# Hybrid attention and short-convolution layer: turned value groups at other steps, another order of the attention step on three engines, and several waits and transfers moved

## The chip, the cores and the metric

The kernel runs on one core of one Trainium2 chip. The metric is device time in microseconds (us): before the change the median of three runs is 2747.36 us (2747.1 to 2748.34). A core has five engines with a queue each, which meet only at semaphores: TensorE (PE) multiplies matrices and turns tiles, VectorE (DVE), ScalarE (ACT) and GpSimd (POOL) work on rows, SyncE (SP) issues most transfers. Each engine takes its instructions in the order of its own program; what is late at the head of a queue holds back all behind it.

## The reference

```python
u = rms_norm(x, norm_mix_g)                       # x: (1, 2048, 1024) float32
q, k, v, bg, cg, hv = split(u @ w_in)             # each 512 wide
s = q_c @ k_c.T + bias[bucket(k_pos - q_pos)]     # 4 heads, 2 halves c of 64 columns each
a = softmax(s_0) - lam * softmax(s_1)
att = rms_norm(a @ v, subln_g) * (1 - 0.2)
conv = bg * short_conv(cg * hv, conv_w)           # width 3 over positions
x = x + concat(att, conv) @ w_out
z = rms_norm(x, norm_ffn_g)
x = x + (silu(z @ w_gate) * (z @ w_up)) @ w_down  # 2816 wide
out = rms_norm(x, final_g)
```

All is float32 within a tight bound. The kernel gets it from products of a rounded type: each operand is split into a high part (a copy that rounds, on ACT) and a low part (operand minus high part, on DVE), and a product is three matmuls: high by high, high by low, low by high.

## The kernel before

It has five stages, one after another on PE.

- **Input projection.** x is normalized in four blocks of 512 rows; each block has four tiles of 128 rows, which `scale_x` scales on DVE, `turn_u` turns on PE, and `split_u` splits on ACT and DVE. Between them stand the first three pieces of the product (`first_product`); `norm_block` is DVE's order within a block. Three further triples of 128 columns follow in a loop (q, k and v), then 4 loops for the convolution. `piece_staged` counts the pieces that DVE has taken out of a bank of PSUM (the memory PE writes to). Near the start the vector of relative bias is spread over the partitions, one matmul for each head (`spread_bias`), and kept by ACT (`keep_bias`).
- **Attention.** 64 steps, 16 for each of 4 heads, counted from 0; step t brings a tile of 128 queries to 2048 keys. In the tables that set the order within a step (one line for steps t % 4 = 0, 1, 2, 3; one table each for PE, ACT and DVE), `s0` to `s3` are the four score units of tile t on PE (4 matmuls of 512 columns each; the two halves of the keys for each of the two halves of a head), `S0` is the first unit of the next tile, `b0` to `b3` add the bias and keep the running minimum on DVE, `x0` and `x1` take the exponential of a 2048 wide row on ACT (`x1` of the tile before), `r` is a reciprocal on DVE. Then POOL scales and adds the two halves (`mixed_ready`). Two steps later the mixed tile is turned in four groups of 128x512 (`g0` to `g3`): 4 transposes on PE, the high part on ACT, the low part on DVE, in two banks of PSUM in turn, so that a group must be finished on DVE before the next but one can start on PE (`group_lo`). The values of a block of four tiles are multiplied in eight parts, `e0` to `e7`, of 6 matmuls each, in steps 1, 2 and 3 after that block; step 0 has none. `o`, `M`, `h`, `R` and `a` normalize a block. `step_groups` says which groups are turned in a step. Four of the groups of a head are its values v instead (tile `None`): quarter 0 in step 2, 1 in step 3, 2 in step 4, 3 in step 5, each behind the step's other groups.
- **Output projection.** 16 tiles of 128 rows (n = 0 to 15). SP loads the mixed tile n (`load_m`, two slots), ACT and DVE split it, PE multiplies, DVE adds x (`add_rows`), ACT squares, POOL takes the root, DVE scales (`norm_rows`), PE turns the result (`turn_z`) one tile later. `norm_rows(n)` stands behind `split_m(n + 2)` on DVE, and so does the square on ACT.
- **Gate and up**, 44 steps of 7 products with sums of blocks.
- **Down and final norm.** Four groups of 512 rows; each sums 22 chunks. `split_down` splits a chunk, `add_y`, `mean_y` and `norm_y` finish the rows, POOL stores them.

The steps around the change in code: `pe.wait_ge(piece_staged, ...)` ahead of the loops over triples and over the convolution; `dve.wait_ge(out_gain_loaded, 16)` ahead of the last product; `load_m` in SP's loop over n.

## Time and profile before

| | |
|---|---|
| median of three runs | 2747.36 us |
| the profiled execution, its own time | 2750.09 us |
| its span (first to last instruction) | 2748.1 us |
| TensorE's mean granted clock | 0.989 |
| input projection | 0 to about 568 us |
| attention | about 568 to 1205 us |
| output projection | about 1200 to 1405 us |
| gate and up | about 1405 to 2243 us |
| down and final norm | about 2243 to 2748 us |
| matmuls | 12280 |

All times below are of the one profiled execution, counted from the start of its span; its own time is 2.7 us over the median. A duration of PE is modelled and includes what overlaps with the next matmul, so what PE costs is read from the distance between starts. "[3.2 <-DVE x]" at the end of a line is how long the engine stood idle before it and what released it. PEclk is the share of full speed that TensorE's clock was granted.

### The profile page before, as it was taken

What the parts mean: (1) busy time and instruction counts of PE and PEld (TensorE: products, weight loads), DVE (VectorE), ACT (ScalarE), POOL (GpSimd) and SP (SyncE); (2) the same over time, 40 slices, a digit from 0 to 9 for tenths busy, and PEclk for the clock granted to TensorE, in tenths of its full rate; (3) what the DMA queues carried; (4) which work ended last, traced back from release to release, by engine and by line L of the source; (5) the groups of instructions that cost most, each with busy time, mean ns of one, the idle gap of its engine ahead of it and who ended that gap; (6) DMA issues with size and microseconds to landing.
All of it is one profiled execution on the core that took longest, in us unless ns stands there. A gap on an engine that the chain in (4) does not pass through costs nothing. (4 is left out here: it accounts for less than half of the span.)

```text
span 2748.1 us, 34348 instructions
## 1 busy us (share of the span) xinstructions
PE 2656.5 (97%) x12280; PEld 2177.7 (79%) x12280; DVE 1505.5 (55%) x2203; ACT 1020.8 (37%) x1429; POOL 501.1 (18%) x343
## 2 busy tenths in 40 slices
PE   7999999989999999999999999999999989999997
PEld 6788888867777777778888888878888878888886
DVE  5311122268878877854476656686666643534343
ACT  5210000047667766742243333343333322323232
POOL 1000000047777777720000000000000000000000
PEclk9999999999999999999999999999999999999999
DMA  6542111223031221047673222352222234556563
GB/s 183 147 126 82 58 38 38 61 62 75 25 76 47 62 61 31 24 146 222 216 232 115 76 84 91 103 165 73 88 85 79 88 123 137 183 172 201 155 200 113
DMA packets 260688, 298.30 MB, mean 109 GB/s; under 512 B 15200, under 2 KB 179552, under 8 KB 260608
## 3 DMA queue, kind: packets, MB, share of 16 engines
q1 hardware_dynamic: 255952, 287.24, 35.2%
q0 software_dynamic: 2304, 8.39, 0.7%
q10 hardware_dynamic: 2352, 1.64, 0.2%
q8 instruction: 46, 0.75, 0.1%
q14 instruction: 34, 0.28, 0.0%
HBM read 212.28 MB, written 84.93 MB: 108 GB/s over the span
## 5 line engine op out<-in xcount | busy, mean ns | idle before, releaser
L1826 PE MATMUL banks<-z_hi,w_hi 128*128 128x512 f32 x1116 | 434.5, 389 | 1.8 <-DVE u L1417 1.1
L1826 PE MATMUL banks<-z_hi,w_lo 128*128 128x512 f32 x1116 | 434.2, 389 | 0.0
L1826 PE MATMUL banks<-z_lo,w_hi 128*128 128x512 f32 x1116 | 434.2, 389 | 0.0
L1621 PE MATMUL projected<-u_t_hi,w_part_hi 128*128 128x512 f32 (+1 forms) x768 | 300.6, 391 | 3.2 <-DVE conv_y L1146 1.7
L1621 PE MATMUL projected<-u_t_lo,w_part_hi 128*128 128x512 f32 (+1 forms) x768 | 299.7, 390 | 0.0
L1621 PE MATMUL projected<-u_t_hi,w_part_lo 128*128 128x512 f32 (+1 forms) x768 | 299.6, 390 | 0.0
L719 POOL TENSOR_TENSOR exp<-exp,exp 128x2048 f32<-128x2048 f32 x64 | 295.5, 4617 | 5.3
L878 ACT ACTIVATE exp<-exp,neg_max 128x2048 f32<-128x2048 f32 x128 | 257.2, 2009 | 36.4 <-DVE neg_max L1288 35.3
L748 POOL TENSOR_TENSOR y_rstd<-y_mean,neg_half 128x1 f32<-128x1 f32 x16 | 8.7, 546 | 1319.5 <-DVE y_mean L1572 1319.5
L1826 PEld LDWEIGHTS banks<-z_hi,w_hi 128*128 128x128 f32 x1116 | 209.5, 188 | 46.9 <-issue 2.8
L1826 PEld LDWEIGHTS banks<-z_lo,w_hi 128*128 128x128 f32 x1116 | 209.5, 188 | 43.3
L1826 PEld LDWEIGHTS banks<-z_hi,w_lo 128*128 128x128 f32 x1116 | 209.5, 188 | 43.3
L980 ACT ACTIVATE w_hi<-w_sum 128x512 fp32r<-128x512 f32 x176 | 110.8, 632 | 328.1 <-PE banks L1826 321.1
L1883 PE MATMUL banks<-down_hi,hid_hi 128*128 128x512 f32 x704 | 217.9, 391 | 7.5 <-DVE down_lo L1560 7.5
L1883 PE MATMUL banks<-down_lo,hid_hi 128*128 128x512 f32 x704 | 217.7, 390 | 0.0
L1883 PE MATMUL banks<-down_hi,hid_lo 128*128 128x512 f32 x704 | 217.5, 390 | 0.0
L888 ACT ACTIVATE a_t_hi<-tile_turned 128x512 fp32r<-128x512 f32 x256 | 148.5, 601 | 157.9 <-PE tile_turned L1713 157.4
L1300 DVE TENSOR_TENSOR a_t_lo<-tile_turned,a_t_hi 128x512 fp32r<-128x512 f32 x256 | 172.1, 687 | 54.0 <-ACT a_t_hi L888 53.9
L1557 DVE TENSOR_TENSOR hid_lo<-hid_raw,hid_hi 128x512 fp32r<-128x512 f32 x88 | 60.9, 693 | 254.3 <-ACT hid_hi L1078 241.8
L1695 PE MATMUL scores<-k_sum,q_part_hi 128*128 128x512 f32 x512 | 178.8, 431 | 15.1 <-DVE neg_max L1288 8.5
L1288 DVE CUSTOM_DVE_ANT_0 exp<-scores,window,half_min 128x1024 f32<-128x1024 f32 x128 | 163.8, 1280 | 31.5 <-PE scores L1695 25.7
L1078 ACT ACTIVATE hid_hi<-hid_raw 128x512 fp32r<-128x512 f32 x88 | 55.5, 631 | 329.9 <-PE banks L1883 329.9
(154 smaller groups left out, 4557.1 us busy)
## 6 DMA issues: line engine op xcount, KB each, us to landing
down_raw<-in_w_down SPq DMA_DIRECT2D x88, 512.0 KB, 4.4
gate_raw<-in_w_gate SPq DMA_DIRECT2D x44, 512.0 KB, 4.8
up_raw<-in_w_up SPq DMA_DIRECT2D x44, 512.0 KB, 5.8
hidden_t<-hid_stage SPq DMA_DIRECT2D x88, 256.0 KB, 2.6
hid_raw<-hidden_t SPq DMA_DIRECT2D x88, 256.0 KB, 3.6
w_raw<-in_w_in SPq DMA_DIRECT2D x24, 512.0 KB, 5.1
projected_t<-stage SPq DMA_DIRECT2D x48, 256.0 KB, 2.5
q_part_hi<-projected_t SPq DMA_DIRECT2D x32, 256.0 KB, 4.5
```

The source lines that it names most:

```text
L719: nc.gpsimd.tensor_tensor(exp_0[:, slot_0], exp_0[:, slot_0], exp_1[:, slot_1], ALU.add).then_inc(mixed_ready, 1)
L878: nc.scalar.activation(rows, rows, ACT.Exp, scale=-1.0, bias=neg_max[:, t % 2, part:part + 1], accum_out=exp_sum[:, part, t % 16:t % 16 + ...
L888: nc.scalar.activation(dst, turned_bank(h, t, index), ACT.Copy).then_inc(group_hi, 1)
L980: nc.scalar.activation(w_slot[k][0][:, :, :], src, ACT.Copy).then_inc(w_hi_ready_2, 1)
L1078: nc.scalar.activation(hid_part[slot][0][:, :], hid_raw[:, slot], ACT.Copy).then_inc(f_hi_ready, 1)
L1288: nc.vector.tensor_tensor_reduce(out=rows[:, half * HALF:(half + 1) * HALF], in0=scores[:, unit % 2], in1=window[:, window_slice(t, half)] ...
L1300: nc.vector.tensor_tensor(parts[1][at], turned_bank(h, t, index), parts[0][at].bitcast(FP32), ALU.subtract).then_inc(group_lo, 1)
L1557: nc.vector.tensor_tensor(hid_part[slot][1][:, :], hid_raw[:, slot], hid_part[slot][0][:, :].bitcast(FP32), ALU.subtract).then_inc(f_lo_re ...
L1621: last = nc.tensor.matmul(projected[:, bank * BANK:(bank + 1) * BANK], w_part[w][:, r if w else HI_SLOT[r], kt], u_t[u][:, kt, rows], star ...
L1695: last = nc.tensor.matmul(scores[:, unit % 2, b * BANK:(b + 1) * BANK], q_part[n][:, (t // 4) % 2, part, t % 4 * P:(t % 4 + 1) * P], k_sum ...
L1826: last = nc.tensor.matmul(c_bank[BANK_OF[k]], w_slot[k][w][:, kt], block[z][:, kt], start=(kt == 0 and t == 0 and k < 4), stop=(kt == 3 an ...
L1883: last = nc.tensor.matmul(y_banks[j][:, c * BANK:(c + 1) * BANK], hid_part[slot][h][:, j * P:(j + 1) * P], down_part[slot][w][:, c * BANK: ...
```

## The change

Attention (steps counted from 0): the values of a head are turned in steps 2 (quarters 0 and 1), 5 and 6; the three order tables are new, with the next tile's first score unit at the end of every step, and a value part in step 7 waits for the last quarter. Input projection: the gain is loaded ahead of the bias table; three of the four bias spreads stand behind the first product; DVE scales the third and fourth tile ahead of taking out pieces; PE's two waits for all pieces become waits for the piece whose bank is needed. Output projection: one tile is loaded in each turn instead of two in every other. Final norm: the wait for the gain moves behind the first group; the last four tiles are finished interleaved, and SP stores them instead of POOL.

ACT, in attention: from the square of a block's sums (`o_sq`, in a step t % 4 = 0) to the end of the next step. exp_82 and exp_74 are the rows of `x1` and `x0`. Before:

```order
L912 ACTIVATE o_sq<-o_sum 128x512
L888 ACTIVATE a_t_hi<-tile_turned 128x4x128
L878 ACTIVATE exp_74,exp_sum<-exp_74,neg_max 128x2048
L888 ACTIVATE a_t_hi<-tile_turned 128x4x128 x2
L878 ACTIVATE exp_82,exp_sum<-exp_82,neg_max 128x2048
L888 ACTIVATE a_t_hi<-tile_turned 128x4x128 x3
L878 ACTIVATE exp_74,exp_sum<-exp_74,neg_max 128x2048
L888 ACTIVATE a_t_hi<-tile_turned 128x4x128
```

The same place of the changed kernel:

```order
L922 ACTIVATE o_sq<-o_sum 128x512
L898 ACTIVATE a_t_hi<-tile_turned 128x4x128 x2
L888 ACTIVATE exp_74,exp_sum<-exp_74,neg_max 128x2048
L898 ACTIVATE a_t_hi<-tile_turned 128x4x128
L888 ACTIVATE exp_82,exp_sum<-exp_82,neg_max 128x2048
L898 ACTIVATE a_t_hi<-tile_turned 128x4x128 x3
L888 ACTIVATE exp_74,exp_sum<-exp_74,neg_max 128x2048
```

The first row of exponentials of step 1 (exp_82) stood ahead of the step's groups; now it stands behind the first of them. The second (exp_74) of steps 0 and 1 has moved to the end of its step.

PE, in attention, the end of a step t % 4 = 2 in which quarters of the values are turned, and the start of the next. Before, in a head's step 2 (k_sum and q_part are the operands of the scores):

```order
L1713 MATMUL tile_turned<-identity,exp_74 128x128 x4
L1759 MATMUL o_norm<-identity,head_rstd 128x128 x4
L1713 MATMUL tile_turned<-identity,v_stage 128x128 x4
L1695 MATMUL scores<-k_sum,q_part_hi 128x512 x2
L1695 MATMUL scores<-k_sum,q_part_lo 128x512 x2
```

Now:

```order
L1732 MATMUL tile_turned<-identity,exp_74 128x128 x4
L1714 MATMUL scores<-k_sum,q_part_hi 128x512 x2
L1714 MATMUL scores<-k_sum,q_part_lo 128x512 x2
L1778 MATMUL o_norm<-identity,head_rstd 128x128 x4
L1732 MATMUL tile_turned<-identity,v_stage 128x128 x8
L1732 MATMUL tile_turned<-identity,exp_74 128x128 x8
```

Four groups of four transposes now follow one another, where one stood between the matmuls of two products.

DVE, the end of the program: the last four tiles. Before:

```order
L1567 TENSOR_TENSOR y_rows<-banks,y_rows 128x1024 x4
L1572 TENSOR_SCALAR y_mean<-y_sumsq 128x1
L1577 SCALAR_TENSOR_TENSOR y_rows<-y_rows,y_rstd,out_gain 128x1024
L1572 TENSOR_SCALAR y_mean<-y_sumsq 128x1
L1577 SCALAR_TENSOR_TENSOR y_rows<-y_rows,y_rstd,out_gain 128x1024
L1572 TENSOR_SCALAR y_mean<-y_sumsq 128x1
```

Now:

```order
L1577 TENSOR_TENSOR y_rows<-banks,y_rows 128x1024 x2
L1582 TENSOR_SCALAR y_mean<-y_sumsq 128x1
L1577 TENSOR_TENSOR y_rows<-banks,y_rows 128x1024
L1582 TENSOR_SCALAR y_mean<-y_sumsq 128x1
L1577 TENSOR_TENSOR y_rows<-banks,y_rows 128x1024
L1587 SCALAR_TENSOR_TENSOR y_rows<-y_rows,y_rstd,out_gain 128x1024
L1582 TENSOR_SCALAR y_mean<-y_sumsq 128x1
```

A mean now stands ahead of the sum or the scaling of another tile, where each mean stood directly ahead of the scaling that waits for it.

```diff
@@ step_groups
-            if t % 16 in (2, 3, 4, 5) and exists(h, t):
-                groups.append((None, t % 16 - 2))
+            if exists(h, t):
+                groups += [(None, q) for q in {2: (0, 1), 5: (2,), 6: (3,)}.get(t % 16, ())]
@@ the order tables (one line of each)
-        PE_ORDER = ("s1 g0 g1 s2 s3 g2 g3 M",
+        PE_ORDER = ("s1 g0 g1 s2 g2 s3 g3 M S0",
...
-        ACT_ORDER = ("x1 g0 o g1 x0 g2 g3",
+        ACT_ORDER = ("x1 g0 g1 o g2 g3 x0",
...
@@ semaphores
+        last_stored = [sem(f"last_stored_{i}") for i in range(4)]
@@ sync: for n in range(N_ROWS)
-                if n % 2 == 0 and n + 2 < N_ROWS:
-                    load_m(n + 2)
+                if n == 0:
+                    load_m(2)
+                if n + 3 < N_ROWS:
                     load_m(n + 3)
@@ sync: the end
-            for j in range(8):
+            for n in range(12, 16):
+                sp.wait_ge(out_ready, n + 1)
+                sp.dma_start(out[0, n * P:(n + 1) * P, :], y_rows[:, n % 8]).then_inc(last_stored[n - 12], 16)
+            for j in range(4):
                 sp.wait_ge(out_stored[j], 32)
+                sp.wait_ge(out_stored[4 + j], 16)
+                sp.wait_ge(last_stored[j], 16)
@@ gpsimd: for group in range(4), between the rsqrts and the stores
+                if group == 3:
+                    continue
@@ scalar: start
+            act.dma_start(mix_gain[:, :], norm_mix_g[0:1, :].to_broadcast([P, D])).then_inc(gain_loaded, 16)
             act.dma_start(rel_sb[:, :], rel_bias).then_inc(rel_loaded, 16)
             act.dma_start(onehot[:, :], bucket_onehot).then_inc(rel_loaded, 16)
-            act.dma_start(mix_gain[:, :], norm_mix_g[0:1, :].to_broadcast([P, D])).then_inc(gain_loaded, 16)
...
             split_u(0, 3)
-            keep_bias(1)
             split_weights(0, 1)
...
                 if first:
-                    keep_bias(2)
-                    keep_bias(3)
+                    for h in range(1, HEADS):
+                        keep_bias(h)
@@ vector: norm_block
                 mean(sb, 2)
+                scale_x(sb, 2)
+                split_u(sb, 0)
+                mean(sb, 3)
+                split_u(sb, 1)
+                scale_x(sb, 3)
                 if 2 in pieces:
                     split_first(sb - 2, 2)
                 if 0 in pieces:
                     split_first(sb - 1, 0)
-                split_u(sb, 0)
-                scale_x(sb, 2)
-                mean(sb, 3)
-                split_u(sb, 1)
-                scale_x(sb, 3)
+                split_u(sb, 2)
                 if 1 in pieces:
                     split_first(sb - 1, 1)
-                split_u(sb, 2)
                 split_u(sb, 3)
@@ vector: last product
-            dve.wait_ge(out_gain_loaded, 16)
             for group in range(4):
+                if group == 1:
+                    dve.wait_ge(out_gain_loaded, 16)
...
-                for j in range(4):
-                    add_y(group, j)
-                if group < 3:
+                    for j in range(4):
+                        add_y(group, j)
                     split_down(group + 1, 1, 1)
-            for j in range(4):
-                mean_y(3, j)
-                norm_y(3, j)
+            add_y(3, 0)
+            add_y(3, 1)
+            mean_y(3, 0)
+            add_y(3, 2)
+            mean_y(3, 1)
+            add_y(3, 3)
+            norm_y(3, 0)
+            mean_y(3, 2)
+            norm_y(3, 1)
+            mean_y(3, 3)
+            norm_y(3, 2)
+            norm_y(3, 3)
@@ tensor: start
-            spread_bias(1)
             pe.wait_ge(bias_out, 2)
             first_product(0, 0)
-            spread_bias(2)
-            spread_bias(3)
+            for h in range(1, HEADS):
+                spread_bias(h)
@@ tensor: between the loops of the input projection
-            pe.wait_ge(piece_staged, 3 + 12)
...
-                        pe.wait_ge(piece_staged, 12 * t + 4 * r + sb)
+                        pe.wait_ge(piece_staged, 12 * t + 4 * r + sb + (1 if r == 0 and sb < 3 else 0))
                         product(sb, r, slice(sb * BANK, (sb + 1) * BANK))
-            pe.wait_ge(piece_staged, 3 + 12 * QKV_TRIPLES)
...
+                        if r == 0:
+                            pe.wait_ge(piece_staged, 12 * QKV_TRIPLES + sb)
                         pe.wait_ge(conv_evacuated, 12 * g + 4 * r + sb + 1)
@@ tensor: attention_step, before a value part
-                        if t % 4 == 2:
+                        if t % 4 == 2 or t % 16 == 7:
                             pe.wait_ge(group_lo, 2 + groups_before(h, t))
```

## Rows read from the trace of the kernel before

**Rows 1.** the profile's page: engines; groups: busy us, mean ns | idle before

```profile
PE 2656.5 (97%) x12280; PEld 2177.7 (79%) x12280; DVE 1505.5 (55%) x2203; ACT 1020.8 (37%) x1429; POOL 501.1 (18%) x343
...
L888 ACT ACTIVATE a_t_hi<-tile_turned 128x512 fp32r<-128x512 f32 x256 | 148.5, 601 | 157.9 <-PE tile_turned L1713 157.4
L1300 DVE TENSOR_TENSOR a_t_lo<-tile_turned,a_t_hi 128x512 fp32r<-128x512 f32 x256 | 172.1, 687 | 54.0 <-ACT a_t_hi L888 53.9
```

**Rows 2.** waits of TensorE's matmuls: engine line <- releaser: us in total, times, longest

```profile
PE tile_turned L1713 <- DVE a_t_lo L1300: 15.3, 14, 2.4
PE tile_turned L1713 <- POOL exp L719: 11.9, 13, 3.3
PE scores L1695 <- DVE neg_max L1288: 8.5, 19, 1.2
...
PE u_turned L1630 <- DVE u_tile L1135: 3.5, 3, 1.3
...
PE projected L1621 <- DVE conv_y L1146: 1.7, 1, 1.7
PE projected L1621 <- DVE stage L1223: 1.1, 1, 1.1
```

**Rows 3.** timeline, start of the last product; start, us, engine line, [idle <- releaser]

```profile
2260.05 0.69 DVE L1557 TENSOR_TENSOR hid_lo<-hid_raw,hid_hi 128x512 fp32r<-128x512 f32 x1 [12.54 <-DMA out_gain<-in_final_g]
...
2261.93 1.22 PE L1883 MATMUL banks<-down_hi,hid_hi 128*128 128x512 f32 x2 [6.88 <-DVE down_lo L1560]
```

**Rows 4.** busy time, just after: us, PE PEld DVE ACT POOL, PEclk, DMA

```profile
2262.00:2267.00 5.00, 5.00 (x12) 3.93 (x13) 1.61 (x2) 0.00 (x0) 0.00 (x0) 0.50 0.68 210
```

**Rows 5.** timeline, output projection: SP's turn n = 12, and what follows

```profile
1364.16 0.45 SPq L521 DMA_DIRECT2D m_raw<-att_t  x1
...
1370.81 1.06 ACT L941 ACTIVATE m_part_hi<-m_raw 128x1024 fp32r<-128x1024 f32 x1 [4.83 <-DMA m_raw<-projected_t]
...
1373.84 1.28 DVE L1369 SCALAR_TENSOR_TENSOR z_tile<-rows,row_rstd,ffn_gain 128x1024 f32<-128x1024 f32 x1 [0.65 <-POOL row_rstd L738]
...
1375.17 1.09 PE L1800 MATMUL banks<-identity,z_tile 128*128 128x128 f32 x8 [2.66 <-DVE z_tile L1369]
```

**Rows 6.** busy time by stretch, just after

```profile
1376.00:1379.60 3.60, 3.60 (x12) 2.83 (x11) 3.57 (x4) 0.00 (x0) 0.00 (x0) 0.53 0.94 282
```

**Rows 7.** timeline, the last 20 us

```profile
2734.45 1.28 DVE L1577 SCALAR_TENSOR_TENSOR y_rows<-y_rows,y_rstd,out_gain 128x1024 f32<-128x1024 f32 x1 [0.68 <-POOL y_rstd L748]
...
2740.38 2.19 POOL L752 DMA_DIRECT2D out<-y_rows  x4
2740.46 1.28 DVE L1577 SCALAR_TENSOR_TENSOR y_rows<-y_rows,y_rstd,out_gain 128x1024 f32<-128x1024 f32 x1 [0.66 <-POOL y_rstd L748]
```

**Rows 8.** busy time by stretch, four steps of attention each, one core

```profile
833.96:871.03 37.07, 35.93 (x195) 28.90 (x194) 30.36 (x55) 26.17 (x35) 28.94 (x18) 1.00 0.20 51
871.04:909.55 38.51, 36.34 (x199) 29.33 (x197) 31.33 (x56) 28.84 (x39) 28.04 (x18) 1.00 0.15 35
909.55:950.89 41.34, 37.59 (x208) 30.24 (x206) 32.58 (x58) 27.64 (x38) 29.80 (x18) 1.00 0.17 45
754.18:796.92 42.74, 39.09 (x207) 31.49 (x206) 32.58 (x58) 27.74 (x38) 29.75 (x18) 0.96 0.16 44
```

**Rows 9.** timeline, steps 12 and 13 of the second head

```profile
835.00 2.01 ACT L878 ACTIVATE exp<-exp,neg_max 128x2048 f32<-128x2048 f32 x1
...
837.23 0.16 DVE L1318 RECIPROCAL recip<-exp_sum 128x1 f32<-128x1 f32 x1
...
844.36 1.09 PE L1713 MATMUL tile_turned<-identity,exp 128*128 128x128 f32 x8 [0.58 <-POOL exp L719]
...
845.21 0.72 PE L1695 MATMUL scores<-k_sum,q_part_hi 128*128 128x512 f32 x2
```

**Rows 10.** timeline, end of step 4 of the second head

```profile
765.17 1.06 PE L1713 MATMUL tile_turned<-identity,v_stage 128*128 128x128 f32 x4 [1.65 <-DVE a_t_lo L1300]
```

**Rows 11.** busy time by stretch, input projection, products of 512 columns alone

```profile
206.00:550.00 344.00, 342.94 (x1513) 283.72 (x1512) 80.81 (x88) 18.95 (x20) 0.00 (x0) 1.00 0.19 55
```

More of the change, by code:

```diff
@@ L223, in build @@
         K_LOAD_STEPS = (8, 9, 11, 12)
-        PE_ORDER = ("s1 g0 g1 s2 s3 g2 g3 M",
[3 rows of a table removed]
-        ACT_ORDER = ("x1 g0 o g1 x0 g2 g3",
-                     "x1 g0 g1 g2 x0 g3",
-                     "x1 g0 g1 x0 g2",
-                     "x1 g0 g1 g2 x0 g3 g4")
+        PE_ORDER = ("s1 g0 g1 s2 g2 s3 g3 M S0",
[3 rows of a table added]
+        ACT_ORDER = ("x1 g0 g1 o g2 g3 x0",
+                     "g0 x1 g1 g2 g3 x0",
+                     "x1 g0 x0 g1 g2",
+                     "g0 x1 g1 g2 x0 g3 g4")
         DVE_ORDER = ("b0 r b1 g0 g1 b2 b3 g2 g3",
[3 rows of a table removed]
[3 rows of a table added]
         back_psum = ExitStack()
```

12 rows, old and new, of tables (DVE_ORDER, PE_ORDER) are left out of this document.

## The prediction

> **What bounds the kernel now.** I read the page first: TensorE is busy 97% of the span [rows 1], so what can be won is what it waits for, and the half clock that a wait brings on. Then the waits of its matmuls [rows 2]: few are long in sum, and they lie in four places. In attention it waits for VectorE's low parts (15.3 us), for GpSimd's mixed tile (11.9) and for scores taken away (8.5); near the start for a scaled tile (3.5); between the loops of the input projection once for each of two loops (1.7 and 1.1). Then the timelines around the two long single waits: 6.88 us at the start of the last product, for a gain that nothing needs yet [rows 3], and 2.66 us in the output projection [rows 5]. After each, the stretch shows TensorE at the lower of its two levels, 1.2 GHz: PEclk 0.50 over 5.0 us [rows 4] and 0.53 over 3.6 us [rows 6]. Last the end, where one chain of small steps runs with TensorE idle [rows 7], and attention by blocks of four steps [rows 8].
>
> **The change part by part.** The sum is made against the profiled execution (2750.1 us; the median is 2.7 lower), and then taken off the median.
>
> *Gain of the last norm.* VectorE stood 12.54 us at the gain and TensorE 6.88 us behind it [rows 3]. Moved behind the first group, the wait has more than 100 us of cover. What is late next: the third chunk is there, since its low part could start as the gain came, and the fifth chunk's loads are issued behind the gain's in the same queue; the gain landed at about 2260.0, TensorE would need the fifth chunk at about 2265.6 (2261.93 less 7.3, plus two chunks of 24 products at 0.227 us, 344.0 us / 1513 [rows 11]), and its load and splits need some 5 us: just enough. I take 6.9 of wait and, from 2261.93 to 2267, half of 5.1 us of lower clock [rows 4]: **-9.4** (from -5, if the loads are late, to -10).
>
> *One load each turn.* Both loads of tiles 14 and 15 stood behind a wait for a split block and went out at 1364.16; ScalarE split tile 14 at 1370.81, and the scaling of tile 12 stands behind that on VectorE (1373.84), so that TensorE waited 2.66 us [rows 5]. Now tile 14 is asked for one turn earlier, ahead of that wait; it needs only the slot of tile 12, which is free by then. 2.66 us and half of 3.4 us of lower clock [rows 6]: **-4.4** (0, if the queue holds it back elsewhere, to -4.7). In the turns before, each load waits for a slot that is free as SP comes to it, and TensorE had no wait there.
>
> *Waits between the loops of the projection.* A product needs the bank it writes, and that bank was emptied one or two products earlier: 1.7 + 1.1 us [rows 2], **-2.8** (-2 to -3).
>
> *Start.* The earlier gain brings the first scaled tile forward, but the low part of the fourth, which the first product waits for, hangs on the input's own loads; three spreads of the bias now stand between products where one had lain in an idle stretch, an estimated +0.9. The third and fourth tile of a block are scaled some 0.6 us earlier in each of two blocks; of the 3.5 us [rows 2] that is a third. Together **-0.3** (-3.5 to +2).
>
> *The end.* Four scalings, each behind its own mean and root, took 2734.45 to 2740.46, 2.0 us apart, and all four stores left POOL after the last root, at 2740.38, one behind another for 2.19 us [rows 7]. Interleaved, the scalings stand 1.2 us apart: the fourth starts about 2737.5, three us earlier. The stores leave SP one by one as tiles are ready, so that only the last one's 512 KB are left after it, not 2 MB. Of the 6.4 us between the end of the last scaling (2741.7) and that of the span I leave 4.4: **-5.0** (-3 to -6.5).
>
> *Attention, the usual block.* Blocks of four steps without values last 37.07 us [rows 8], of which TensorE's own work is about 34.5: 16 score units and 8 value parts make 112 products at 0.227 us (25.5), 16 turned groups at 0.44 (two of them stand 0.85 apart from the next scores [rows 9], 7.0 in all), and the block's norm, an estimated 2. The bound is a chain that leaves TensorE: x1 at 835.00 takes 2.0 us, the reciprocal stands at 837.23, and 7.13 us of GpSimd later the first group starts (844.36), after a wait of 0.58 [rows 9]. Through the step without value products TensorE has only some 9 us of work beside these 11.2. The new order does not shorten the chain there: the value part e7 is put between the last scores and the last two groups of a step t % 4 = 3, but ScalarE takes x1 behind these groups, so that x1 comes later by the same 1.37 us. In steps 1 and 3 x1 now stands behind the step's first group, so it can't start before that group is turned and copied (0.60 us on ScalarE [rows 1] after about as long on the way). Followed with the durations of [rows 9]: first group of step 3, +1.2, +2.0, +0.1, +7.1 gives the first group of the next step 0 at +10.5, and one more pass of GpSimd (7.3) the first group of step 1 at +17.8; step 3's first group stands at 18.7 after that of step 1. The cycle is 36.5 us instead of 37.07: -0.55 in each of eight blocks, **-4.4** (bounds -2.5 each, all of the waits, and +1.0 each, if a second step joins the chain).
>
> *Attention, the heads' first blocks.* Values turned in steps 2 and 3 made the block 38.51, those in 4 and 5 made it 41.34 or 42.74 [rows 8]; in step 4 the group waited 1.65 us, and the clock fell right behind [rows 10]. Now step 4 is a usual one. Two quarters at the end of step 2, with two groups after them, must pass two banks: each group needs about 0.6 us to ScalarE, 0.60 there and 0.69 on VectorE [rows 1] before its bank is free, so the third starts 1.2 us late. With 0.9 us of own work and that wait the block gets 2 us longer than a new usual one with a head's 0.9 for filling the bias window: 39.4 against 38.51, **+2.7** in three heads. Blocks 4 to 7: step 5's quarter is followed at once by a value part that waits for it (1.5 us), step 6's costs about one more: 36.5 and 3.6, 40.1 us, against the 42.0 that the two rows average: **-7.6** over four heads. The first eight steps, where a score unit now stands ahead of the wait for the first mixed tile, and the last steps, where e0 fills a wait: **-2.5**.
>
> Sum: 9.4 + 4.4 + 2.8 + 0.3 + 5.0 + 4.4 - 2.7 + 7.6 + 2.5 = 33.7 us less; 2747.4 - 33.7 = **2714 us**.
>
> The runs of transposes raise one question. In the row, the clock fell just after TensorE had turned tiles, multiplied one column and stood for 1.65 us [rows 10]; this alone doesn't tell whether turning counts as work. The Trainium skill (TensorE: Matmul & The Clock Gate, Part 4: PE-mode transpose) says that full clock "doesn't engage" for transposes. By that rule the five groups in a row at the end of step 2 may bring the clock down once in each head; at 1.7 us a fall, as in [rows 6], that would be 2720 at most. The sum above counts neither falls lost nor won in attention.
>
> **The rivals.**
> *A, attention gains far more.* The chain may have slack that I don't see (the row shows only 0.58 us of wait for GpSimd; the other waits of that block are VectorE's), and orders on all three engines changed together. With 1.5 us more in each of twelve usual or near-usual blocks: 2696. Against it: GpSimd is busy 28.9 of 37.07 us [rows 8], and r waits for x1 in each step.
> *B, attention gains nothing.* x1 behind the first group costs in steps 1 and 3 what the fuller step 0 returns, and the two quarters in step 2 stall longer. Then only the other parts are left, 21.9 us: 2725; with 3 us lost, 2728.
> *C, slower than before.* The same mechanism, in all steps: each first group starts x1, x1 starts GpSimd, and GpSimd starts the next step's first group, at 10.5 us a step where a block now takes 9.3 a step. It decides once a usual block is over 37.07 + 21.9/16 = 38.4 us; at four steps of 10.5 it would be 42, and the kernel about 2747 + 16 x 5 - 22 = 2805. Against it: in steps 1 and 2 TensorE has more than 10.5 us of its own between first groups.
> *D, the waits only move.* With the gain's wait gone, the fifth chunk's loads are late by as much, and the final stores are bound by bandwidth: 9 us less gain, 2723.
>
> **How the numbers follow.** Forecast 2714 with 0.50 (its own range 2706 to 2721); A 0.15; B 0.22; D 0.08; C 0.03; a mix of small losses that leaves no change 0.02. The range takes in B and most of A: 2698 to 2730. About 0.2% (5.5 us) is what a measurement of this kernel can tell from no change. Faster by more: 0.50 + 0.15 + 0.22 + 0.08 = 0.95; within: 0.02; slower: 0.03.
>
> **What would show it.** Right: no wait for the gain and full clock from 2243 on; no wait at the turn of tile 12; last scaling about 3 us before it stood, stores on SP's queue, about 5 us from there to the end; usual blocks of 36 to 37 us, with the wait for GpSimd at the first groups of steps 0 and 1; a head's first block near 39.4 and second near 40. Wrong: usual blocks under 35.5 us (A) or over 37.1 (B, C), first groups 10.5 us apart in every step (C), a wait for a chunk's load in the first group of the last product (D).

## The result and the profile after

The changed kernel takes 2732.17 us (median of six runs, 2730.52 to 2732.73); the kernel before took 2747.85 us beside it. The ratio is 0.994 (0.9927 to 0.9953): 15.7 us or 0.6% faster, not the 33 us of the forecast, and 2 us above the upper end of its range. The profiled execution lasted 2732.24 us, its span 2730.3.

The stages, each measured from the first matmul of its kind to the first of the next (us):

| | before | after | difference | forecast |
|---|---|---|---|---|
| start and input projection | 568.78 | 573.66 | +4.9 | -3.1 |
| attention | 638.67 | 635.96 | -2.7 | -11.8 |
| output projection | 193.75 | 189.25 | -4.5 | -4.4 |
| gate and up | 842.64 | 842.64 | 0.0 | 0 |
| down, to the last matmul | 488.22 | 478.63 | -9.6 | -9.4 |
| last matmul to the end | 16.07 | 10.13 | -5.9 | -5.0 |

The lower half came as forecast. Two rows miss 17.1 us: 8.0 at the start, 9.1 in attention; the others gave 1.2 more than forecast. The column "before" is of an execution 2.7 us over its median; experiment *a_old* shows that attention misses more than this table says.

What answers to [rows 1], the page: TensorE is still busy 97% of the span.

```profile
PE 2645.6 (97%) x12280; PEld 2176.8 (80%) x12280; DVE 1507.3 (55%) x2203; ACT 1017.0 (37%) x1429; POOL 499.8 (18%) x339
...
L898 ACT ACTIVATE a_t_hi<-tile_turned 128x512 fp32r<-128x512 f32 x256 | 147.5, 595 | 169.5 <-PE tile_turned L1732 167.5
```

What answers to [rows 2], the waits of TensorE's matmuls (total, times, longest):

```profile
PE tile_turned L1732 <- POOL exp L727: 24.4, 33, 3.2
PE projected L1634 <- DVE rel_wide L1125: 9.1, 1, 9.1
PE tile_turned L1732 <- DVE a_t_lo L1310: 8.9, 18, 1.6
PE u_turned L1650 <- DVE u_tile L1145: 8.0, 7, 2.1
PE tile_turned L1732 <- DVE v_part_lo L1310: 7.7, 8, 1.1
PE o_sum L1739 <- DVE v_part_lo L1310: 5.7, 4, 1.4
...
PE scores L1714 <- DVE neg_max L1298: 1.2, 5, 0.2
...
PE scores L1714 <- DVE half_min L1298: 0.5, 1, 0.5
```

The scores had a second wait before, of nearly the same size as the one in [rows 2]:

```profile
PE scores L1695 <- DVE half_min L1288: 6.4, 17, 0.5
```

The waits for score banks are nearly gone (8.5 and 6.4 to 1.2 and 0.5), those between the projection loops quite. In their place stand twice the wait for GpSimd (11.9 to 24.4) and waits for the values' low parts (7.7 + 5.7, where 1.9 stood before). Summed over this view, the matmuls of attention waited 44 us before and 49 after: the waits moved and did not shrink. At the start the wait for scaled tiles is 8.0 instead of 3.5. The first wait, for rel_wide (9.1, before 6.6), is longer because the bias table is now loaded behind the gain; by *s_all_old* and *s_norm_old* below this costs the stage nothing that can be told.

The turn of tile 12 in the output projection, which answers to [rows 5, 6]: VectorE scales it at 1369.59, TensorE turns it at 1374.53 without a wait, and the clock stays full (1.00).

```profile
1369.59 1.28 DVE L1379 SCALAR_TENSOR_TENSOR z_tile<-rows,row_rstd,ffn_gain 128x1024 f32<-128x1024 f32 x1 [0.66 <-POOL row_rstd L746]
```

```profile
1374.53 1.03 PE L1819 MATMUL banks<-identity,z_tile 128*128 128x128 f32 x8
```

```profile
1370.00:1376.00 6.00, 6.00 (x32) 5.08 (x31) 5.97 (x7) 1.92 (x1) 0.00 (x0) 1.00 1.13 335
```

The start of the last product, which answers to [rows 3, 4]: 0.59 us of wait at its first matmul, and then 20.49 us of work in 20.50 at full clock (PEclk, the third figure from the end, is 1.00). The wait of 6.88 us and its half clock are gone; the fifth chunk was not late.

```profile
2241.51 0.73 PE L1902 MATMUL banks<-down_hi,hid_hi 128*128 128x512 f32 x2 [0.59 <-DVE down_lo L1570]
```

```profile
2241.50:2262.00 20.50, 20.49 (x90) 16.99 (x91) 8.36 (x10) 5.49 (x7) 0.00 (x0) 1.00 0.85 295
```

The end, which answers to [rows 7]. The last matmul starts at 2720.14. The last two scalings follow one another from 2724.67; SP has sent the first tile off at 2723.01.

```profile
2721.70 1.28 DVE L1587 SCALAR_TENSOR_TENSOR y_rows<-y_rows,y_rstd,out_gain 128x1024 f32<-128x1024 f32 x1
...
2722.96 1.27 DVE L1587 SCALAR_TENSOR_TENSOR y_rows<-y_rows,y_rstd,out_gain 128x1024 f32<-128x1024 f32 x1
2723.01 4.50 SPq L695 DMA_DIRECT2D out<-y_rows  x4
...
2724.67 2.48 DVE L1587 SCALAR_TENSOR_TENSOR y_rows<-y_rows,y_rstd,out_gain 128x1024 f32<-128x1024 f32 x2 [0.37 <-POOL y_rstd L756]
```

Attention, which answers to [rows 8]: a head's first block (40.20, before 38.51), its second (40.49, before 41.34 or 42.74), a usual one (36.69, before 37.07).

```profile
873.98:914.18 40.20, 36.51 (x203) 29.93 (x202) 31.89 (x58) 29.16 (x40) 28.90 (x18) 1.00 0.14 32
914.18:954.67 40.49, 36.79 (x204) 29.92 (x202) 31.88 (x56) 26.96 (x37) 28.92 (x18) 1.00 0.18 48
991.34:1028.03 36.69, 35.38 (x196) 29.10 (x194) 30.71 (x56) 25.88 (x35) 28.94 (x18) 1.00 0.20 51
```

PEclk is 1.00 in the first of these rows, which holds the turned groups that follow one another at the end of step 2: TensorE's clock did not fall for the run of transposes in heads 1, 2 and 3 (first blocks of 40.25, 40.20 and 40.21 us, all at 1.00), against what the forecast weighed from the Trainium skill (TensorE: Matmul & The Clock Gate, Part 4: PE-mode transpose). In head 0 it had fallen earlier in step 2, in a wait for GpSimd of 3.15 us, and was full again through the run. The run is four groups, not the forecast's five, and is broken by the wait of 1.07 us that experiment *v_spread* is about. Scores stand on both sides of it, so this does not show whether turning counts as work.

The start. SP takes x's tiles for the third block in line behind the stores of the pieces before; the squares of ScalarE wait for these loads. Before:

```profile
42.11 0.68 DVE L1146 TENSOR_TENSOR conv_y<-projected,stage 128x512 fp32r<-128x512 f32 x1
...
44.02 10.75 SPq L369 DMA_DIRECT2D x_tile<-in_x  x4
48.81 1.06 ACT L774 ACTIVATE conv_y<-x_tile 128x1024 f32<-128x1024 f32 x1 [4.40 <-DMA x_tile<-in_x]
```

```profile
70.30 1.06 ACT L774 ACTIVATE conv_y<-x_tile 128x1024 f32<-128x1024 f32 x1 [4.10 <-DMA x_tile<-in_x]
```

After:

```profile
45.39 0.68 DVE L1156 TENSOR_TENSOR conv_y<-projected,stage 128x512 fp32r<-128x512 f32 x1
...
46.10 0.33 SPq L390 DMA_DIRECT2D projected_t<-stage  x1
46.47 0.43 SPq L391 DMA_DIRECT2D projected_qk_lo_t<-conv_y  x1
47.30 11.63 SPq L371 DMA_DIRECT2D x_tile<-in_x  x4
52.95 1.06 ACT L785 ACTIVATE conv_y<-x_tile 128x1024 f32<-128x1024 f32 x1 [7.01 <-DMA x_tile<-in_x]
```

```profile
79.19 1.06 ACT L785 ACTIVATE conv_y<-x_tile 128x1024 f32<-128x1024 f32 x1 [8.74 <-DMA x_tile<-in_x]
```

VectorE takes out the second piece of the first block 3.3 us later (45.39 against 42.11), its store follows, and the loads for the third block start 3.3 us later, directly behind it. The squares of the fourth block stand 8.9 us later (79.19 against 70.30).

### The profile page after: what moved, and what is told of

It reads as the page before. It is cut to its first block and busy times, and to the rows that moved or that the text cites. A ratio compares the mean times of both kernels' runs of the same rounds, so it can differ in the third digit from the quotient of the medians.

```text
span 2730.3 us, 34351 instructions
## 1 busy us (share of the span) xinstructions
PE 2645.6 (97%) x12280; PEld 2176.8 (80%) x12280; DVE 1507.3 (55%) x2203; ACT 1017.0 (37%) x1429; POOL 499.8 (18%) x339
## 5 line engine op out<-in xcount | busy, mean ns | idle before, releaser
L1732 PE MATMUL tile_turned<-identity,exp 128*128 128x128 f32 x1024 | 145.9, 281 | 40.9 <-POOL exp L727 24.4
L1732 PEld LDWEIGHTS tile_turned<-identity,exp 128*128 128x128 f32 x1024 | 119.5, 143 | 77.3 <-POOL exp L727 37.9
```

Source lines behind the costliest of these rows:

```text
L1732: last = nc.tensor.transpose(turned_bank(h, t, index)[:, i], src, identity[:, :])
```

## The experiments

Where a stage is named, it is measured as in the table above. "Base" is the kernel of *s_stores_late*. The kernel before took 2747.8 to 2748.8 us (medians) beside these runs. A stage scatters even where its code is the same. In the nine kernels that share the start of the base the first score unit stands at 564.2 to 566.1 us. In the five that share the changed attention (the changed kernel, *s_all_old*, *s_norm_old*, *s_stores_late*, *end_pool*) that stage takes 635.0 to 636.9. So a difference of 1 or 2 us in one of these stages is not put down to an edit here. In these five the blocks of heads 1 to 3 repeat within 0.1 us, so blocks are compared where it matters.

### What the start lost

*s_all_old* undoes the three start edits of the change (order of VectorE's block, place of the bias spreads, place of the gain's load). *s_norm_old* undoes only the first:

```diff
                 mean(sb, 2)
-                scale_x(sb, 2)
-                split_u(sb, 0)
-                mean(sb, 3)
-                split_u(sb, 1)
-                scale_x(sb, 3)
                 if 2 in pieces:
                     split_first(sb - 2, 2)
                 if 0 in pieces:
                     split_first(sb - 1, 0)
+                split_u(sb, 0)
+                scale_x(sb, 2)
+                mean(sb, 3)
+                split_u(sb, 1)
+                scale_x(sb, 3)
...
```

> The changed kernel with all three start edits undone: the gain loaded last, one bias spread ahead of the first product, pieces taken out between the scalings as before. Theory 1 (the start's new order costs, the new waits between loops gain): first score unit at about 566 us (changed kernel 573.7, before 568.8), total about 2725 (0.9915 of before). Rival (the 5 us come from the new waits between loops or from the loops themselves): still about 573, total 2732.

> The changed kernel with only VectorE's order in a normalized block put back (pieces taken out between the scalings). Theory 1 (nearly all of the loss at the start comes from this order, through late stores and loads on SyncE's queue): first score unit at about 568 us, 5 to 6 us earlier than in the changed kernel, total about 2726.5. Rival (the bias spreads and the late bias table cost it): first score unit at 572 to 573, total 2731.

Measured: *s_all_old* 2726.55 us (ratio 0.9921, 0.9904 to 0.9938), first score unit at 566.48; *s_norm_old* 2725.15 us (0.9916, 0.9899 to 0.9933), at 566.71. Theory 1 holds: VectorE's order alone costs 7.0 us (573.66 to 566.71), and the other two start edits differ by 0.2 us, which is within the scatter. (*s_all_old* is 1.4 us the slower of the two in all; its attention, of the same code, took 636.59 us against 635.03.) Against the kernel before, what is left with the old start is -2.3: the waits between the loops, forecast at -2.8.

*s_stores_late* leaves VectorE's new order and moves SP's stores:

```diff
-            next_block(0, True)
-            with sp.Fori(1, SB - 1) as sb:
-                next_block(sb, False)
+            for j in range(4):
+                load_x(1, j)
+            for sb in range(1, SB):
+                for j in range(4):
+                    if sb + 1 < SB:
+                        load_x(sb + 1, j)
+                    if j == 1:
+                        if sb > 1:
+                            store_first(sb - 2, 2)
+                        store_first(sb - 1, 0)
+                        store_first(sb - 1, 1)
```

> The changed kernel with SyncE's stores of a block's first pieces placed behind the first two loads of the block after the next, ahead of its other two; VectorE's order stays the new one. Theory 1 (loads stand behind stores that wait for pieces taken out late): the squares of the third and fourth block no longer wait 7 and 9 us for their loads, first score unit at 569 to 570, total about 2728. Rival (VectorE's own order holds TensorE, not the queue): 573 or later, total 2732 or more; later still if the stores now hold ScalarE's next pieces.

Measured: 2724.74 us (0.9912, 0.9896 to 0.9929), first score unit at 565.48, 8.2 us earlier than in the changed kernel and 3.3 earlier than before. With the same order on VectorE the loss is gone, so the order costs time only through SP's queue: the pieces are taken out later, their stores stand in line later, and behind them the loads. The loads for the third block now start at 40.28, and the fourth block's squares wait at most 0.73 us:

```profile
66.77 1.05 ACT L793 ACTIVATE conv_y<-x_tile 128x1024 f32<-128x1024 f32 x1
...
68.64 1.06 ACT L793 ACTIVATE conv_y<-x_tile 128x1024 f32<-128x1024 f32 x1 [0.73 <-DMA x_tile<-in_x]
```

It gave 4 us more than theory 1 said: in this kernel the fourth block's squares also stand 3.5 us ahead of where they stood before the change (66.77 against 70.30), when they waited 4.1 us for their load. *v_tables_norm_old* tried both cures at once (on *v_old_tables*, below):

> The fastest so far (2719.6: old tables, new steps of the values, SyncE's stores behind the next loads) with VectorE's old order in a normalized block as well. If late stores hold the start: the old order adds little, first score unit at 564.5 to 566.5 (565.9 before), total 2719 to 2720. Rival (both cures add up): 563 or less, total 2717.

Measured: 2721.74 us (0.9905, 0.9888 to 0.9923), first score unit at 566.90 against 565.87. The cures do not add. The old order even makes the whole kernel 2.1 us slower than *v_old_tables*; 1.0 of it shows at the start, which is within the scatter.

### What attention gained

*a_old* is the changed kernel with attention as before: the three tables, the values' steps, the wait in step 7.

> The changed kernel with attention as before: tables, turned values in steps 2, 3, 4 and 5, and the wait in step 7. If attention's own gain is the 2.7 us that the two profiles show: attention 638.5 us long, total about 2735. Rival (attention gained more, and what stands ahead of it took that back, as by another state of the queues at its start): attention over 640 us, total 2737 or more.

Measured: 2732.39 us (0.9943, 0.9926 to 0.9959): the same time as the changed kernel. Attention lasts 635.18 us, 0.8 less than with the new one. So the change to attention is worth nothing that can be told from the scatter; the 2.7 us in the table are not its work, and neither theory had that. Where they come from shows in a head's second block, whose instructions and waits are the same as before:

```profile
757.61:798.91 41.30, 37.56 (x207) 30.22 (x205) 32.59 (x58) 27.64 (x38) 29.79 (x18) 1.00 0.16 45
```

```profile
768.60 0.63 PE L1732 MATMUL tile_turned<-identity,v_stage 128*128 128x128 f32 x4 [1.66 <-DVE a_t_lo L1310]
```

The same block took 42.74 at PEclk 0.96 in the kernel before [rows 8], with the same wait, 1.65 us [rows 10]. The wait stands; the clock fell after it in one execution and not in the other. Three heads differ so: the second blocks of heads 0, 1 and 3 took 42.07, 42.74 and 43.03 us at 0.96 before, and 40.66, 41.30 and 41.68 at 1.00 in *a_old*. That is 4.2 us, more than the 3.5 between the two attentions.

Two edits make up the change to attention, and two kernels part them, both on the base. *v_old_steps* puts the values' steps back, *v_old_tables* the tables:

```diff
-                groups += [(None, q) for q in {2: (0, 1), 5: (2,), 6: (3,)}.get(t % 16, ())]
+                groups += [(None, q) for q in {2: (0,), 3: (1,), 4: (2,), 5: (3,)}.get(t % 16, ())]
```

```diff
-        PE_ORDER = ("s1 g0 g1 s2 g2 s3 g3 M S0",
+        PE_ORDER = ("s1 g0 g1 s2 s3 g2 g3 M",
...
```

> Base: the changed kernel with SyncE's stores behind the next loads (2724.7). Only the values' steps put back: quarters in steps 2, 3, 4, 5 with the new tables. Theory (the new steps cost the heads' first blocks what they give the second): a head's first block 38.2 (40.2 in the base), its second 42 (40.5), usual blocks 36.67; attention within 1 us of the base's 636.9, total 2724 to 2725. Rival (the tables alone make the long first block): first block stays at 40, second 42, attention 640, total 2728.

> Same base, with the three old order tables and the new steps of the values. Theory (usual blocks are the tables' gain, 0.38 each in 9 of them): usual blocks 37.05, first blocks 39.5, second blocks 40.5; attention 638, total 2726. Rival (the placement does not matter, the tables do all): first 38.5, second 41.3, as with both undone; attention 635.5.

Measured: *v_old_steps* 2723.99 us (0.9912, 0.9896 to 0.9929), *v_old_tables* 2719.61 us (0.9896, 0.9879 to 0.9912). All four combinations, in us (blocks typical of heads 1 to 3; *a_old* has the start of the changed kernel, the others that of the base):

| tables, steps | attention | first block | second | usual |
|---|---|---|---|---|
| old, old (*a_old*) | 635.2 | 38.5 | 41.3 | 37.05 |
| old, new (*v_old_tables*) | 631.8 | 39.3 | 39.5 | 37.05 |
| new, old (*v_old_steps*) | 635.1 | 39.7 | 41.3 | 36.66 |
| new, new (base) | 636.9 | 40.2 | 40.5 | 36.67 |

The new steps gain 3.4 us with the old tables. With the new ones attention is 1.8 longer, but that is the size of the scatter: first and second block together fall from 81.0 to 80.7, the whole kernel is 0.75 us slower, and the rest lies in the first eight and the last steps. The new tables make the usual block 0.38 shorter. The blocks with values are 0.9 to 1.2 us longer with them, save the second with the old steps, which stays. I had expected the first block at 38.2 with the old steps, it is 39.7; and the total of the old tables 6 us too high. *v_2356* moved one quarter from step 2 to step 3:

```diff
-                groups += [(None, q) for q in {2: (0, 1), 5: (2,), 6: (3,)}.get(t % 16, ())]
+                groups += [(None, q) for q in {2: (0,), 3: (1,), 5: (2,), 6: (3,)}.get(t % 16, ())]
```

> Same base, new tables, quarters in steps 2, 3, 5, 6: the second quarter moves from step 2, where it makes five groups in a row, to step 3. Theory (the five groups in a row wait for two banks): first block 38.5 to 39.2 instead of 40.2, nothing else moves; attention 632 to 635, total 2720 to 2723. Rival (step 3 has five groups already; a sixth waits as long as the fifth of step 2 did): first block 40 or more, total 2725.

Measured: 2727.32 us (0.9923, 0.9906 to 0.9939), attention 639.6. Theory and rival both missed. The first block falls only to 39.7, and the second rises to 42.1: in step 3 the quarter costs 1.6 us of its own (it stands behind the next tile's first score unit, and so counts in the second block). By the distances between first score units, a quarter alone in step 2, 3, 5 or 6 costs 1.6 to 2.2 us in the new tables, and two together in step 2 cost 2.2. What it waits for is in the trace of the changed kernel, at the end of a head's step 2: the quarter is the last thing in its step, behind `R`, and the next step opens with groups again.

```profile
904.81 0.60 PE L1732 MATMUL tile_turned<-identity,v_stage 128*128 128x128 f32 x4
906.48 1.16 PE L1732 MATMUL tile_turned<-identity,exp 128*128 128x128 f32 x8 [1.07 <-DVE v_part_lo L1310]
```

In the old tables the next step opens with a score unit, four matmuls of cover. *v_spread* therefore puts the quarters among the products (base otherwise):

```diff
-                    "s1 g0 g1 s2 e0 s3 g2 g3 e1 e2 S0",
-                    "e3 s1 g0 g1 s2 e4 s3 e5 g2 S0 R",
+                    "s1 g0 g1 s2 e0 s3 g2 g3 e1 g4 e2 S0",
+                    "e3 s1 g0 g1 s2 e4 s3 e5 g2 g3 S0 g4 R",
```

> Base: the changed kernel with SyncE's stores behind the next loads (2724.7). New tables and new steps of the values, but a quarter stands among the step's products instead of behind the last score unit: in step 5 between e1 and e2, in steps 2 and 6 behind e5 (the second one of step 2 behind the next tile's first score unit). Theory (a quarter costs 1.7 to 2.1 us in the new tables only because it is the last thing in its step, so that the next value part or group waits for two banks; its own work is 0.44): a head's second block 38.0 to 38.5 instead of 40.5, its first 39 to 39.5 instead of 40.2, usual blocks 36.67; attention 626 to 629, total 2714 to 2717. Rival (the fifth group of a step costs as much wherever it stands, since ScalarE and VectorE are late): second block 40 or more, total 2723 or more.

Measured: **2713.95 us** (0.9876, 0.9858 to 0.9894), attention 626.2. The theory holds. It is the fastest kernel that computes the whole result, 18.2 us under the changed one. First block 39.73, second 38.22, usual 36.64:

```profile
861.18:900.91 39.73, 36.72 (x203) 29.87 (x202) 32.00 (x58) 29.25 (x40) 28.98 (x18) 1.00 0.14 33
900.91:939.13 38.22, 36.68 (x204) 29.82 (x202) 32.09 (x56) 26.96 (x37) 28.87 (x18) 1.00 0.19 51
975.79:1012.43 36.64, 35.35 (x196) 29.09 (x194) 30.73 (x56) 25.89 (x35) 28.94 (x18) 1.00 0.20 51
```

TensorE's waits for the values' low parts, 7.7 + 5.7 us in the base as in the changed kernel, are down to 0.6. A quarter in the second block now costs 0.8 us instead of 1.9. Only the first block stayed a little over what was expected (39 to 39.5).

### What a usual block waits for

My forecast had a chain: x1, the reciprocal, GpSimd, the next first group. *v_x1_first* puts x1 first again in steps 1 and 3; *v_x1_r_first* the reciprocal as well.

```diff
-                     "g0 x1 g1 g2 g3 x0",
+                     "x1 g0 g1 g2 g3 x0",
```

> Same base, with ScalarE's x1 put first again in steps t % 4 = 1 and 3, the rest of the new tables kept. Theory of the chain (the cycle is bound by x1, the reciprocal, GpSimd and the next first group): the waits for GpSimd ahead of the first groups of steps 0 and 1 (0.88 and 0.48 us) shrink and a usual block falls to 35.4 to 36.2; attention 12 us shorter at best, total 2713 to 2720. Rival (the banks of the turned groups bind as well, and a copy 2 us later costs as much): 36.7 or more, total 2724 to 2735.

> The base of v_x1_first, with VectorE's reciprocal of steps t % 4 = 1 and 3 also put directly behind the first bias addition. v_x1_first left the waits for GpSimd as they were (0.9 and 0.46 us), since the reciprocal stood behind the first group's low part. Theory of the chain (the reciprocal's place, not x1's, sets GpSimd's start): the two waits shrink or go, usual blocks 36.2 to 36.8. Rival (VectorE standing at the reciprocal for x1 holds the score banks): usual blocks 37.4 or more, the wait behind the second score unit of step 1 over 1 us.

Measured: 2740.9 us (0.9976, 0.9966 to 0.9986) and 2739.36 us (0.9968, 0.9956 to 0.998): 16.2 and 14.6 us slower than the base. Usual blocks 37.4 to 37.9, and 37.4. In *v_x1_r_first* one further block has a fallen clock (45.0 us at 0.92), in *v_x1_first* none behind head 0. A usual block of *v_x1_first*:

```profile
994.12:1031.56 37.44, 35.41 (x195) 29.10 (x194) 30.39 (x56) 25.63 (x35) 28.90 (x18) 1.00 0.19 50
```

With x1 first in ScalarE's queue, the first group of step 1 is copied 1.5 us after TensorE starts it instead of 0.7, and its low part is late. Behind the third score unit stands the first value part, which waits for that low part: 0.80 us, in the base 0.05.

```profile
1007.02 0.50 PE L1747 MATMUL o_sum<-a_t_hi,v_part_hi 128*128 128x512 f32 x1 [0.80 <-DVE a_t_lo L1318]
```

The waits for GpSimd in that block stayed (0.77 and 0.30 us, in the base 0.73 and 0.32). With the reciprocal moved too, the one in step 0 goes, as the chain's theory said, but the third group of the same step then waits 0.85 us for VectorE's low part, and the first value part of step 1 still waits 0.79. So the chain binds, but the low parts of the turned groups bind just behind it. The wait that the rival foresaw, over 1 us for the score banks, did not appear. Does GpSimd's length bind at all? *v_pool_short* shortens it (on *v_spread*):

```diff
-                    nc.gpsimd.tensor_tensor(exp_0[:, slot_0], exp_0[:, slot_0], exp_1[:, slot_1], ALU.add).then_inc(mixed_ready, 1)
+                    nc.gpsimd.tensor_tensor(exp_0[:, slot_0, 0:1024], exp_0[:, slot_0, 0:1024], exp_1[:, slot_1, 0:1024], ALU.add).then_inc(mixed_ready, 1)
```

> v_spread with GpSimd adding only the first 1024 of the 2048 columns of the two halves (the other half of the sum is left out), so that its pass takes some 2.3 us less in each step. Theory (GpSimd's chain is the last thing a usual block waits for): the waits ahead of the first groups of steps 0 and 1 (0.88 and 0.48 us) go, usual blocks 35.2 to 35.4 instead of 36.66. Rival (behind GpSimd stands another wait of the same length, the score banks or the copies): 36.0 or more.

Measured: 2700.25 us (0.9827, 0.9798 to 0.9855); attention 615.0, usual blocks 36.13. The rival holds, narrowly: it had asked for 36.0 or more. Step 0 of a usual block in *v_spread*, and then the same in *v_pool_short*, TensorE's matmuls:

```profile
978.60 1.09 PE L1740 MATMUL tile_turned<-identity,exp 128*128 128x128 f32 x8 [0.73 <-POOL exp L735]
...
980.81 0.66 PE L1740 MATMUL tile_turned<-identity,exp 128*128 128x128 f32 x4 [0.19 <-DVE a_t_lo L1318]
```

```profile
968.60 1.03 PE L1740 MATMUL tile_turned<-identity,exp 128*128 128x128 f32 x8
...
971.69 0.66 PE L1740 MATMUL tile_turned<-identity,exp 128*128 128x128 f32 x4 [0.86 <-DVE a_t_lo L1318]
```

The wait for GpSimd (0.73) is gone, and the third group of the same step waits 0.86 for VectorE's low part instead of 0.19: what was won ahead of the first group is lost ahead of the third. Only step 1 keeps its gain (10.50 to 9.96 us from score to score), 0.5 us, where GpSimd's addition fell from 4.62 to 2.40 us in each pass.

*v_pe_only* (on *v_spread*) puts back the tables of ScalarE and VectorE alone.

> v_spread with ScalarE's and VectorE's order tables of before; only TensorE's table is new. If TensorE's order brings the gain: usual blocks 36.6 to 36.8. Rival (it needs the order on the other two): usual blocks 37.1 or more; a head's second block longer as well.

Measured: 2722.44 us (0.9907, 0.9879 to 0.9936), usual blocks 37.57 us: 0.5 worse than all old, 0.9 worse than all new; the second block is longer as well (38.6 against 38.2). The rival holds: TensorE's order alone gains nothing there. (Attention as a whole, 633.7 us, is 1.5 us shorter than in *a_old*, which turns the values at the old steps and outside the products.)

What the new tables bring a usual block shows in the distances between the starts of TensorE's matmuls (steps 8 to 11 of head 2, *a_old* against the base). What is lost ahead of scores falls from 2.2 to 0.9 us, what is lost ahead of turned groups and value parts rises from 1.0 to 1.9. The rest, TensorE's own work, is 33.8 us in both.

### What the end gained

*end_pool* is the changed kernel with the last four stores back on POOL:

```diff
-                if group == 3:
-
-                    continue
```

> The changed kernel with the last four stores back on POOL, behind its last root; VectorE's interleaved order stays. From the last matmul to the end it is 10.1 us in the changed kernel and 16.1 before. Theory (the interleaving gives 3 us of the 5.9, the stores one by one on SyncE the rest): 12.5 to 13.5, total about 2735. Rival (the chain alone, the transfers are hidden): 10 to 10.5, total 2732; or the stores alone: 15 to 16, total 2738.

Measured: 2734.8 us (0.9955, 0.9937 to 0.9972), last matmul to the end 12.75 us against 10.13 and 16.07 (from the last matmul to the span's end). Interleaving gave 3.3 us, the stores on SP 2.6.

## Why the prediction was wrong, by its own steps

The forecast was 18 us short. At the start 8.0 are missing, and in attention, with *a_old* as the measure, 12.6; the other terms gave 1.2 more. Two steps failed: the start's term, which left out a queue, and the term of the heads' blocks with values, which had a gain where there was a loss.

- **Gain of the last norm, -9.4:** right, -9.6, with both halves (wait and clock). **One load each turn, -4.4:** right, -4.5. **The end, -5.0:** -5.9, in the two parts it named; after the last scaling 3.1 us were left, not 4.4. **Waits between the loops, -2.8:** -2.3, by *s_all_old*.
- **Start, -0.3 (-3.5 to +2):** wrong, +7.2 (4.9 and the 2.3 above). This step failed outright. It counted that the scalings come 0.6 us earlier and never asked what comes later for it: taking out the pieces. Of the work that is moved back, it left out who waits: SP's stores, and in that queue the loads of x behind them. The estimated +0.9 for the bias spreads did not show: they and the gain's place differ by 0.2 together (*s_all_old* against *s_norm_old*).
- **Usual block, 36.5 (-0.55 each):** 36.67, 0.38 shorter than 37.05, so -3.0 for eight. That the size came near is luck in part. The forecast named GpSimd's chain as the only bound: x1 and the reciprocal sooner should then have given more, and *v_x1_r_first* made the block longer, while *v_pool_short* gave 0.5 where 1.4 was expected. Behind GpSimd stands a wait of nearly equal length, for the low parts that free the two banks of turned groups. The 0.38 itself comes from the score banks, whose waits the forecast counted as 8.5 us (with half_min's 6.4 they are 14.9) and took no gain from. Its 11.2 us for the way from x1 to the first group do not follow from its rows either, which give 9.4 (835.00 to 844.36). Which lines of the three tables bring the 0.38 was not parted; TensorE's table alone does not, and ScalarE's x1 put back first loses it.
- **Heads' first blocks, 39.4:** 40.2. **Second blocks, 40.1 against 42.0:** 40.5 against 41.3. The sum had +2.7 and -7.6 for these; by *a_old* they were +5.1 (three of 1.7) and -2.7 (heads 1 to 3; head 0's is the same within 0.1), so that together a gain of 4.9 was in truth a loss of over 2. Two mistakes: the 42.0 averaged a block with a fallen clock (1.4 us of 42.74), which *a_old* loses without the edit; and the cost of a quarter was set too low, for the new tables end a step with the quarter and start the next with another group or a value part (1.9 us each in the second block, 0.8 in *v_spread*, where they do not).
- **First eight and last steps, -2.5:** the first eight steps 72.88 in the changed kernel, 71.24 in *a_old*, the last 0.6 shorter: +1.0. Most of this is the clock in the first four steps, PEclk 0.89 against 0.94: *s_norm_old*, with the changed attention at 0.95, has 71.80. The gain of 2.5 did not come in either.
- **Rival B** (attention gains nothing) came true, with 0.22, and half of its mechanism: the two quarters in step 2 stall longer, but the usual blocks gain a little, which it denied. Its 2725 missed only what the start lost. The range's upper end took in B but no cost of the start over +2.

## What to carry to other kernels

When an instruction is moved up, price the one that it moves down, and follow that one through every queue it feeds: here the subtractions held the stores, the stores the input loads behind them, and that took 7 us. A rule of placement is worth what the order around it makes of it: measure orders and placements in all combinations before keeping either, and don't let the filler be the last thing of a step if the next opens with work that needs the same two banks. And before counting a slow block as an edit's gain, look whether it is slow by its clock, and how far the stage scatters between kernels in which it is the same.

## What was not expected of the hardware

The same wait does not always bring the lower clock. In *v_pool_short* three heads run the same first block; in two it is 40.9 us at PEclk 0.96, in the one between them 39.36 at 1.00:

```profile
702.76:743.70 40.94, 38.05 (x204) 31.32 (x202) 32.10 (x58) 29.12 (x40) 20.15 (x18) 0.96 0.14 32
853.59:892.95 39.36, 36.64 (x204) 30.08 (x201) 31.98 (x57) 29.12 (x40) 20.10 (x18) 1.00 0.14 33
1002.79:1043.70 40.91, 38.17 (x204) 31.40 (x202) 32.09 (x58) 29.12 (x40) 20.13 (x18) 0.96 0.15 31
```

In the first 6.24 us of each of these blocks TensorE was busy 4.15, 4.14 and 4.15 us, and each stretch ends in the same wait of 1.57 us for VectorE's low part. At its end the clock fell to half in the first and the third (at 709.00 and 1009.37), and not in the second. So neither that wait nor TensorE's busy time in this stretch tells the two apart, and the price of a fall, 1.4 to 1.6 us on top of the wait, is paid or not. The kernel before paid it behind the quarter in step 4 in three of four heads, *a_old*, with the same attention 5 us later, in none. Whether an edit far ahead switches it, or it differs from execution to execution, is not shown: the kernel before alone took from 2745.0 to 2751.1 us beside the experiments, with mean granted clocks from 0.989 to 0.993. Two profiles that differ by two or three microseconds in a stage say nothing of an edit until their clocks are compared.
